# Second attention of a three-block transformer on one core: the next head's two long score products issued ahead of the current head's first transposes, with VectorE and ScalarE reordered to match

## What is computed

```python
def mla_attention(q_nope, q_rope, k_nope, k_rope, v, q_chunk_blocks, k_chunk):
    # for each block of 128 queries and each of the 16 heads
    s = (einsum('bqhd,bkhd->bhqk', qn, k_nope)
         + einsum('bqhr,bkr->bhqk', qr, k_rope)).astype(float32) * scale
    p = softmax(where(mask, s, -inf), axis=-1)      # mask: chunk-causal, chunks of 64
    return einsum('bhqk,bkhd->bqhd', p, v)          # then o @ w_o, added to the residual
```

## Time and profile before

| | us |
|---|---|
| median of 3 runs | 2171.34 (2170.37 to 2171.51) |
| the profiled execution: its own time | 2169.1 |
| its span, first to last instruction | 2167.3 |
| TensorE matmul busy | 2089.9 (96%) |
| VectorE, ScalarE, GpSimd busy | 1086.7, 775.9, 1104.6 |
| the second attention with its first scores, 769 to 950 us of the span | 181 |
| TensorE busy in it | 158.24 |

### The profile page before, as it was taken

One profiled execution on the slowest core, in us unless ns is written; L12 is line 12 of the kernel. 1 busy time (PEld: TensorE's weight loads), 2 busy tenths in 40 slices (PEclk: granted clock), 3 DMA queues, 4 the chain that ended last, 5 costly groups with the idle time before them and its releaser, 6 DMA issues.

```text
span 2167.3 us, 38691 instructions
## 1 busy us (share of the span) xinstructions
PE 2089.9 (96%) x13856; PEld 1863.3 (86%) x13856; DVE 1086.7 (50%) x1886; ACT 775.9 (36%) x1286; POOL 1104.6 (51%) x1363
## 2 busy tenths in 40 slices
PE   7999899999999989999999999999999999999997
PEld 6888799999999867789999999877778778888886
DVE  6666745324246656654435336765622364325154
ACT  3443624223123456633412223434432224323232
POOL 5444246555557412135556546753554665656554
PEclk9999999999999999999999999999999999999999
DMA  5222122322333201022332323322232332333332
GB/s 177 69 73 73 59 78 88 100 86 87 98 85 110 79 20 40 21 64 81 95 98 88 96 88 94 105 83 69 82 94 88 107 116 88 97 90 94 98 87 78
DMA packets 51658, 185.42 MB, mean 86 GB/s; under 512 B 5728, under 2 KB 5856, under 8 KB 51552
## 3 DMA queue, kind: packets, MB, share of 16 engines
q1 hardware_dynamic: 50544, 182.02, 27.9%
q10 hardware_dynamic: 1008, 1.89, 0.3%
HBM read 181.79 MB, written 2.10 MB: 85 GB/s over the span
## 4 chain that ended last, share of the span: by engine, by line
PE 89%; DVE 6%; issue 2%; ACT 2%; DMA 0%; DVEq 0%; SPq 0%; ACTq 0%
PE ps L573 27%; PE ps L574 27%; PE ps L575 27%; PE ps L778 2%; PE ps L690 1%; DVE small L1185 1%; PE ps L795 1%; PE ps L721 1%; PE ps L705 1%; PE ps L947 1%; DVE x_hi L991 1%; PE ps L788 1%; DVE scratch L1170 0%; PE ps L637 0%; DVE scratch L1196 0%
## 5 line engine op out<-in xcount | busy, mean ns | idle before, releaser
L552 POOL TENSOR_TENSOR w_lo<-w_raw,w_hi 128x256 fp32r<-128x256 f32 x1356 | 1102.0, 846 | 1038.2 <-ACT w_hi L1549 1024.5
L573 PE MATMUL ps<-x_hi,w_hi 128*128 128x264 f32 (+2 forms) x2704 | 865.7, 320 | 11.9 <-issue 5.4
L574 PE MATMUL ps<-x_lo,w_hi 128*128 128x264 f32 (+2 forms) x2704 | 852.5, 315 | 0.0
L575 PE MATMUL ps<-x_hi,w_lo 128*128 128x264 f32 (+2 forms) x2704 | 851.3, 315 | 0.0
L573 PEld LDWEIGHTS ps<-x_hi,w_hi 128*128 128x128 f32 x2704 | 511.3, 189 | 61.2 <-issue 18.1
L574 PEld LDWEIGHTS ps<-x_lo,w_hi 128*128 128x128 f32 x2704 | 510.7, 189 | 35.1 <-issue 1.5
L575 PEld LDWEIGHTS ps<-x_hi,w_lo 128*128 128x128 f32 x2704 | 510.7, 189 | 32.4
L1549 ACT ACTIVATE w_hi<-w_raw 128x1024 fp32r<-128x1024 f32 x339 | 354.0, 1050 | 317.1 <-PE ps L575 307.9
L573 PE MATMUL ps<-g_hi,w_hi 128*128 128x264 f32 (+2 forms) x1312 | 407.2, 310 | 5.4 <-issue 4.3
L574 PE MATMUL ps<-g_lo,w_hi 128*128 128x264 f32 (+2 forms) x1312 | 405.6, 309 | 0.0
L575 PE MATMUL ps<-g_hi,w_lo 128*128 128x264 f32 (+2 forms) x1312 | 405.2, 309 | 0.0
(11 more groups left out here) (202 smaller groups left out, 1709.0 us busy)
## 6 DMA issues: line engine op xcount, KB each, us to landing
w_raw<-stream SPq DMA_DIRECT2D x339, 512.0 KB, 3.6
h<-x_t SPq DMA_DIRECT2D x4, 528.0 KB, 8.5
out_t<-h SPq DMA_DIRECT2D x8, 256.0 KB, 2.1
scratch<-rotary_tables ACTq DMA_DIRECT2D x4, 264.0 KB, 5.7
par<-params ACTq DMA_DIRECT2D x1, 342.5 KB, 5.3
scratch<-positions ACTq DMA_DIRECT2D x1, 256.0 KB, 2.6
cst<-shape_constants ACTq DMA_DIRECT2D x1, 193.0 KB, 6.8
```

The source lines that it names most:

```text
L552: last = nc.gpsimd.tensor_tensor(w_lo[:, j % 4, cols], w_raw[:, j % 4, cols], w_hi[:, j % 4, cols].bitcast(F32), ALU.subtract)
L573: nc.tensor.matmul(out_ap, w_hi[:, s, c], xh[:, k, cols], start=first, stop=False)
L574: nc.tensor.matmul(out_ap, w_hi[:, s, c], xl[:, k, cols], start=False, stop=False)
L575: return nc.tensor.matmul(out_ap, w_lo[:, s, c], xh[:, k, cols], start=False, stop=last)
```

## The change

Three streams are reordered; no instruction is added or removed. TensorE issues the next head's scores of units 0 and 1 before the current head's transposes of units 0 and 1. VectorE takes the two maxima before it scales units 2 to 4 of the current head. ScalarE alternates: copy of the transposed unit 0, exponential of unit 0, copy of unit 1, exponential of unit 1.

```diff
@@ TensorE, head_b
-                transposes_b(h, 0), transposes_b(h, 1)
                 if more:
                     scores_of_b(h + 1, 0), scores_of_b(h + 1, 1)
-                else:
+                transposes_b(h, 0), transposes_b(h, 1)
+                if not more:
                     pe.wait_ge(o_taken_b, 5 * h)
                 fill(0)
@@ VectorE, head_b
                         take_output_b(h - 1, idx)
-                scale_b(h, (2, 3, 4))
                 if more:
                     maximum_b(h + 1, 0), maximum_b(h + 1, 1)
+                scale_b(h, (2, 3, 4))
@@ ScalarE, head_b
-                take_transposed_b(h, 0), take_transposed_b(h, 1)
+                take_transposed_b(h, 0)
                 if more:
-                    exps_b(h + 1, 0), exps_b(h + 1, 1)
+                    exps_b(h + 1, 0)
+                take_transposed_b(h, 1)
+                if more:
+                    exps_b(h + 1, 1)
```

## The result

The changed kernel takes 2179.24 us (median of 7 runs, 2176.54 to 2179.79) against 2171.34 for the kernel before on the same chip (7 runs, 2168.68 to 2172.58). The ratio is 1.0037, 95% interval 1.0027 to 1.0046: **slower by 8.0 us, between 5.9 and 10.0**. The forecast was 2180.9, in a range of 2175.7 to 2186.0. The span of the profiled execution went from 2167.3 to 2174.8 us, +7.5.

What follows compares the result with a forecast made beforehand. TensorE was taken as busy nearly throughout, with the pace-setting engine differing by head in the second attention. Terms 1.6 + 5.8 + 1.6 + 1.2 - 1.8 + 1.2 = +9.6 us; forecast 2180.9 us, range 2175.7 to 2186.0.

Steps and rivals of the forecast that it cites:

- The mechanism: Second attention: scores still wait for the last output copies; transposes, moved behind, no longer cover them, leaving TensorE idle 1.06 us.
- faster: Rival: transposes, not copies, hold the scores, so all heads move up by up to 1.06 us; about 2157 us, chance 0.04.
- Absorbed: Rival: the moved block falls into small TensorE waits in more heads; +3.6, 2174.9 us, within 0.2%, chance 0.08.
- Colder: Rival: longer idle brings another 3.4 us at 1.2 GHz at all three rotary stalls; +13.5, 2184.8 us, chance 0.15.
- heads 5, 9: Query-piece heads where TensorE sets the pace: block costs 1.06, 0.27 given back, 0.79 each, +1.6 us.
- heads 2, 6, 10 and 3, 7, 11, with their clock: Rotary heads: scalings delay the rotary copies 0.9, then the moved block costs 1.06, three times each; +5.8, clock +1.2.
- heads 4, 8, 12: Key-piece heads where ScalarE sets the pace: the copy between exponentials adds 0.58 each, less 0.1 in head 4; +1.6 us.
- heads 13, 14: Heads with no piece: the block fits in a wait, but ScalarE's chain grows by 0.58 each; +1.2 us.
- heads 0, 1: No output copy holds the scores, so they start earlier; gain between 0.7 (TensorE) and 2.7 (ScalarE), taken as -1.8 us.
- The clock: Rotary stalls: TensorE idle 1.06 longer, head 3 comes to look like head 7, 2.4 us more work at half speed; +1.2.
- The low end: The terms' low ends together, without a clock term: +5.7 us instead of +9.6.
- The slow scalings beside GpSimd: Heads 2 and 4: VectorE's scalings would fall from 2.19 us (head 2) to 0.70, but only 0.1 per head on the path.

Runs made afterwards that it cites:

- e5: The changed kernel with outputs of units 2 to 4 in PSUM bank 7 instead of bank 3: 0.9990 of the kernel before, -2.2 us.
- e7: The kernel before, all orders old, with outputs of units 2 to 4 in bank 7 instead of bank 3: ratio 1.0012, +2.6 us.
- e12: The changed kernel run and profiled again on the same chip: 1.0032 of the kernel before, +6.9 us.
- e8: The kernel before with the new TensorE order (next head's scores ahead of transposes) in head 0 alone: ratio 0.9989, -2.4 us.
- e1: The kernel before with only TensorE's order changed, VectorE and ScalarE as before: ratio 1.0016, +3.5 us.
- e2: The kernel before with only VectorE's order changed, the other engines as before: ratio 1.0016, +3.5 us.
- e9: Kernel before with new TensorE order except in heads 3, 7, 11, and outputs of units 2 to 4 in bank 7: 0.9973, -5.9 us.
- e11: Kernel before, old bank, with head 0's new TensorE order and the query piece ahead of the scores in heads 3, 7, 11: 0.9967, -7.2 us.
- e3: The kernel before with only ScalarE's order changed, the other engines as before: ratio 1.0017, +3.7 us.
- e4: The changed kernel with TensorE's old order kept in heads 3, 7 and 11: 1.0013 of the kernel before, +2.8 us.
- e10: e9 with the query piece of heads 3, 7, 11 also put ahead of the scores: 0.9933 of the kernel before, 2155.93 us, -14.5 us.

## Why the prediction was right, and where it was off

**The mechanism was right.** Idle time of 0.99 us ahead of L778, ended by L1202, with the transposes behind the scores, is what the text named as its proof, and e5 to e7 show that it is a cause and not a symptom. The rival *faster* rested on the transposes, not the copies, holding the scores; the scores start 0.15 us after the copies in both kernels, so it is out. *Absorbed* is out, since heads 5 and 9 pay. *Colder* did not come either: the stretches of heads 7 and 11 stayed at 6.8 us, and no run had a longer one. The terms, against the profiled execution:

| term of the sum | predicted | measured |
|---|---|---|
| heads 5, 9 | +1.6 | +1.5 |
| heads 2, 6, 10 and 3, 7, 11, with their clock | +5.8 + 1.2 | +6.3 |
| heads 4, 8, 12 | +1.6 | +1.2 |
| heads 13, 14 | +1.2 | +1.0 |
| heads 0, 1 | -1.8 | -2.8 |
| sum | +9.6 | +7.1 |

The rest of the +7.5 of the spans, 0.4 us, lies ahead of the first score (769.6 and 770.0 us), where nothing was changed.

**The clock, taken at +1.2, fitted partly by luck.** I looked at the stalls only. There it was near: adding up TensorE's busy time inside the half-clock stretches gives 15.2 us before and 17.1 after, and half of the difference is 0.95 us. But head 0 has such a stretch too, and in the first profile of the changed kernel it was gone, which gives back 1.7. In the second profile (e12) it was there, and the sum over all heads was 21.0 us against 18.6 before, exactly +1.2. So the term is right on one execution and 1.9 too high on the other. Nor do the runs tie it to the longer idle time. e8's stalls are as long as before (3.80, 3.54 and 3.56 us), and yet 20.4 us of TensorE's work fell in the stretches there, against 15.2 in the kernel before. Head 3 did come to look like head 7 as assumed, but it did so in e8 as well. The term belonged in the range, not in the sum.

**Heads 0 and 1, taken at -1.8.** Without the clock the gain is 1.1 (2.8 - 1.7); e12 has 1.4, and e8, with the old order on ScalarE, 1.65 in head 0 and 0.3 in head 1. TensorE's end of my two bounds (0.7) was nearer than ScalarE's (2.7), of which I took most. That error and the clock's stretch went opposite ways.

**The copy between the exponentials, taken at 0.58 (its duration), costs 0.48**, the distance between two starts on ScalarE: 873.83 to 874.31. A copy's duration overlaps the start of the next instruction. That is 0.1 in each of five heads.

**Heads 2, 6, 10 and 3, 7, 11: the route held, though the periods hide it.** The period of head 6 grew by 1.0 in e1 and by nothing in e2, as if TensorE set the pace. But its slip lies inside the next head's wait, as predicted, and what counts is the end of the rotary copies. Counted from the last value product of head 1, 5 or 9, they end 0.58, 0.80 and 0.81 us later than before (predicted 0.8, 0.9 and 0.9), and in head 6 VectorE's order alone gives that 0.80. Behind the wait the moved block costs 1.04, 1.06 and 1.03 us with the clock taken out (predicted 1.06). Together 2.2 + 3.1, and 0.95 for the clock, make the +6.3 of the table.

**The low end** of the sum (+5.7) leaves out that of heads 4, 8 and 12 (0.4 and not 0.58 in each); with it, it is +5.2. The range starts below both.

**The slow scalings beside GpSimd** went from 2.19 us in head 2 to 0.70:

```profile
798.95 0.70 DVE L1196 TENSOR_SCALAR scratch<-scratch,small 128x272 f32<-128x272 f32 x3
```

They no longer run beside GpSimd's four instructions (L552), which ended at 798.07. The first maximum did (797.40) and took its usual 0.71 us. The rule of the Trainium skill, SBUF — State Buffer, Who interferes with whom, that a `tensor_reduce` never contends on trn2, agrees with that. As predicted little of it reached the time: head 4 lost 0.25 where head 8 lost 0.48, so 0.2 and not 0.1. The rule of the Trainium skill, TensorE: Matmul & The Clock Gate, Part 4 (PE-mode transpose), that the full clock does not engage for transposes, again disagrees with the trace: the moved block takes 0.90 us in head 5 (833.70 to 834.60), outside every half-clock stretch.

## What to carry to other kernels

Before work is moved away from where it stands, ask what runs beside it: a block of TensorE work between a product and the next user of its PSUM bank is the cover for the copy out of that bank, and an order is only as good as the bank assignment under it. The same reordering cost 8 us with the outputs in the scores' bank and gained 2 with them in the transposes' bank. Where an engine stands idle for another's chain, work that needs nothing from that chain can be put there (here a projection piece, 2155.9 us). What it brings has to be read from the rows: here the moved work itself gained nothing, since it had been the cover of another chain, and the gain was a shorter time at half clock. Each part of a reordering that spans several engines has to be tried alone: here those of VectorE and ScalarE cost in sum, and that of TensorE gained in one head.

## What the runs showed of the hardware

In the second attention the half-clock stretches were 3.4 or 6.8 us long in every profile. One lay at each of the three stalls in all twelve profiles in which TensorE stood idle there (2.67 to 4.88 us; e9 has the shortest, 2.67 to 2.77). Elsewhere they vanished or changed length in the same head of the same kernel from one execution to the next: head 0, with 2.36 us idle, has none in the first profile of the changed kernel and 3.4 us in the second. Stretches also came without such an idle time. In e11 three of 3.4 us came behind waits of 1.41 us in head 1 and 1.55 us in heads 7 and 11, in e3 and e4 one each in head 14 behind 2.04 and 1.66 us, and in e10 one of 6.8 us behind waits of 1.55 and 0.63 us in head 7 (the row below), while heads 3 and 11 of e10 have the same waits and no stretch.

```profile
857.00:864.00 7.00, 6.75 (x26) 4.91 (x27) 3.73 (x15) 1.58 (x8) 0.00 (x0) 0.51 0.02 8
```

A profile of one execution can thus be off by 1.7 us for each 3.4 us at half clock against another of the same kernel. Differences of this size were read here from the heads without a stretch, or from the ratio of many runs.
